# Two transformer-like blocks in one kernel: TensorE takes part of the expert row sums in the scan and in the routing, and the row units are dealt out anew

## What is computed

```
u = expert_u[eidx]
v = expert_v[eidx]
act = jax.nn.gelu(jnp.einsum('td,thkd->thk', xb, u).astype(jnp.float32), approximate=False)
return jnp.einsum('thk,thkd->td', (g * act).astype(v.dtype), v)
```

```
y_diag = jnp.einsum('blsgr,bsgrp->blgrp', cb[..., None] * decay, xc)
y_off = jnp.einsum('blgn,bgrpn->blgrp', cc, state) * jnp.exp(acum)[..., None]
new_state = (state * jnp.exp(acum[:, -1])[..., None, None]
             + jnp.einsum('blgn,blgr,blgrp->bgrpn', bc, to_end, xc))
```

## Time and profile before

| | |
|---|---|
| median of 3 runs | 3194.34 us (3190.66 to 3200.55) |
| the profiled execution: its time, its span | 3194.24 us, 3192.5 us |
| PE busy in the span | 2254.2 us |
| DVE busy | 1920.1 us |
| POOL busy, 1024 gathers of 0.52 MB | 1288.0 us |
| DMA moved | 807.66 MB, mean 253 GB/s |
| mean granted TensorE clock | 0.841 of 2.4 GHz |

### The profile page before, as it was taken

The page is one execution under the profiler, slowest core; times in us unless marked ns, Lnnn a source line. Parts: engine busy times, 40 slices in busy tenths (PEclk is TensorE's granted clock), DMA queues, the critical chain, the costliest instruction groups (busy, mean ns, idle before and its releaser), DMA issues. The chain is left out here.

```text
span 3192.5 us, 25912 instructions
## 1 busy us (share of the span) xinstructions
PE 2254.2 (71%) x8920; PEld 1652.1 (52%) x8920; DVE 1920.1 (60%) x3629; ACT 485.6 (15%) x1248; POOL 1288.0 (40%) x1058
## 2 busy tenths in 40 slices
PE   6987899753785568775745473135548957797998
PEld 5846788543653557663622362023347426564863
DVE  2317110288988995855799878996876681251000
ACT  3412100111321210001101101011011001231100
POOL 0000000004775464865357887886887550000000
...
GB/s 137 132 79 1 145 158 158 99 53 275 403 402 336 216 356 380 391 389 329 260 244 302 396 411 352 351 291 333 335 409 412 416 407 186 20 2 122 170 144 117
DMA packets 292402, 807.66 MB, mean 253 GB/s; under 512 B 35744, under 2 KB 52128, under 8 KB 292272
## 3 DMA queue, kind: packets, MB, share of 16 engines
...
HBM read 803.84 MB, written 2.10 MB: 252 GB/s over the span
## 5 line engine op out<-in xcount | busy, mean ns | idle before, releaser
L1021 POOL DMA_INDIRECT expert_rows<-in_peer_u,chosen x512 | 673.1, 1315 | 973.7 <-DVE chosen L1522 717.7
L1021 POOL DMA_INDIRECT expert_rows<-in_peer_v,chosen x512 | 611.5, 1194 | 355.0 <-DVE h L1103 143.1
L1093 DVE SCALAR_TENSOR_TENSOR expert_rows<-expert_rows,u 128x1024 f32<-128x1024 f32 x512 | 606.5, 1223 | 71.5 <-DMA expert_rows<-in_peer_u,chosen 65.7
L1103 DVE SCALAR_TENSOR_TENSOR h<-expert_rows,expert_coef,h 128x1024 f32<-128x1024 f32 x240 | 309.1, 1288 | 29.8 <-DMA expert_rows<-in_peer_v,chosen 27.4
L1103 DVE SCALAR_TENSOR_TENSOR u<-expert_rows,expert_coef,u 128x1024 f32<-128x1024 f32 x236 | 304.4, 1290 | 30.3 <-DMA expert_rows<-in_peer_v,chosen 30.0
L573 PE MATMUL product<-uT,in_slab 128*128 128x272 f32 (+1 forms) x1024 | 241.0, 391 | 94.8 <-DMA in_slab<-in_w_in 94.8
L573 PEld LDWEIGHTS product<-uT,in_slab 128*128 128x128 f32 x1024 | 193.6, 193 | 127.2 <-issue 92.6
L2219 PE MATMUL mlp_up<-mlp_xT,mlp_slab 128*128 128x256 f32 x1024 | 227.3, 385 | 16.1 <-DMA mlp_slab<-in_w_up 14.4
L2229 PE MATMUL mlp_down<-mlp_slab,upT 128*128 128x512 f32 x512 | 221.2, 593 | 4.2 <-DMA mlp_slab<-in_w_down 4.2
L2219 PEld LDWEIGHTS mlp_up<-mlp_xT,mlp_slab 128*128 128x128 f32 x1024 | 197.5, 193 | 45.7 <-DMA mlp_slab<-in_w_up 15.9
L1215 PE MATMUL mix_product<-uT,mix_slab 128*128 128x258 f32 (+1 forms) x768 | 173.4, 389 | 15.6 <-DMA mix_slab<-in_w_in 9.1
...
## 6 DMA issues: line engine op xcount, KB each, us to landing
...
```

Of the source, the lines that this page charges most:

```text
L1021: pool.indirect_dma_start(out=self.row(n), out_offset=None, in_=self.tables[0 if dot else 1], in_offset=bass.IndirectOffsetOnAxis(ap=picks ...
L1093: dve.scalar_tensor_tensor(self.row(n), self.row(n), 1.0, u, ALU.mult, ALU.mult, accum_out=dot).then_inc(self.rows_used, 1)
L1103: dve.scalar_tensor_tensor(o, self.row(n), coef, o, ALU.mult, ALU.add).then_inc(self.rows_used, 1)
```

## The change

The units of half 1's first block are dealt out anew: 128 in project (4 at each column tile instead of 3), 128 in scan (8 at each pass instead of 3), 128 in merge instead of 172, 8 in the norm instead of 12, 120 in route. PE takes 48 of the 128 adds of tile 0 (3 of 8, in scan) and 69 of the 128 adds of tile 1 (3 of 8 in the norm and the search, which is 27; then 6 of 8 in the pair search, which is 42), 117 in all instead of 32. The diagonals get six buffers of their own. In scan the two PSUM banks for PE's sums come from `cb` and `grown`: their two buffers now share a bank each, PE does the products with the state before `begin`, and two of its waits are one pass tighter. Half 0's first block and the whole second block keep their order.

```diff
-PLAN_ONE = (140, 60, 172, 12)
+PLAN_ONE = (128, 128, 128, 8)
...
             for n in range(CONV):
                 if bg:
-                    bg.use(dve, 3)
+                    bg.use(dve, 4)
                 dve.wait_ge(tap_ready, n + 1)
...
+        if bg:
+            bg.share_with_tensor(ctx, psum)
         sums = psum(ctx, "sums", [P, 512])
         seg = [psum(ctx, f"seg{i}", [P, HPG, P]) for i in range(2)]
-        cb = [psum(ctx, f"cb{i}", [P, 512]) for i in range(2)]
         yo = [psum(ctx, f"yo{i}", [P, 2, GW]) for i in range(2)]
-        grown = [sums, psum(ctx, "grown", [P, 512])]
+
+        if bg:
+            both = psum(ctx, "cb", [P, 512])
+            cb, grown = [both[:, i * P:(i + 1) * P] for i in range(2)], [sums[:, i * GW:(i + 1) * GW] for i in range(2)]
+        else:
+            cb = [psum(ctx, f"cb{i}", [P, 512])[:, 0:P] for i in range(2)]
+            grown = [x[:, 0:GW] for x in (sums, psum(ctx, "grown", [P, 512]))]
...
                 if q >= 2:
                     square_group(q - 2)
+                if bg:
+                    bg.diagonals(act, SETS_S + SETS_Q * q)
...
                 if bg:
-                    bg.use(dve, 3)
+                    bg.use(dve, SETS_Q)
...
                 if q >= 2:
                     pe.wait_ge(decay_done, q - 1)
                     pe.wait_ge(mixer_ready, q - 1)
+                if bg and q:
+                    pe.wait_ge(mixer_ready, q)
                 at = slice(M + c * P, M + (c + 1) * P)
-                pe.matmul(cb[q % 2][:, 0:P], bf[:, g, at], cf[:, g, at], start=True, stop=True)
+                pe.matmul(cb[q % 2], bf[:, g, at], cf[:, g, at], start=True, stop=True)
...
             for q in range(N + 1):
-                if q + 1 < N:
+                if q + 1 < N and not bg:
                     begin(q + 1)
                 if q < N:
                     c, g = q // GROUPS, q % GROUPS
@@ -949,14 +962,21 @@
 
...
                     if q >= 2:
                         pe.wait_ge(y_ready, q - 1)
-                    if FIRST + max(q - 1, 0):
-                        pe.wait_ge(state_done, FIRST + max(q - 1, 0))
+                    done = q if bg else FIRST + max(q - 1, 0)
+                    if done:
+                        pe.wait_ge(state_done, done)
                     pe.matmul(yo[q % 2][:, 1, :], cf[:, g, M + c * P:M + (c + 1) * P], state[:, g * GW:(g + 1) * GW],
                               start=True, stop=True)
-                    pe.matmul(grown[q % 2][:, 0:GW], bt[:, c, g * STATE:(g + 1) * STATE], product(xend, q),
+                    pe.matmul(grown[q % 2], bt[:, c, g * STATE:(g + 1) * STATE], product(xend, q),
                               start=True, stop=True).then_inc(off_done, 1)
+                if q + 1 < N and bg:
+                    begin(q + 1)
                 if q:
                     inside(q - 1)
+                if bg:
+                    bg.tensor_sums(pe, SETS_S + SETS_Q * q)
+            if bg:
+                bg.tensor_sums(pe, UNITS)
             leave(pe)
 
 UNITS = 2 * TT * SLOTS
...
     RING = 16
-    SHARE = 64
-
-    def __init__(self, nc, t, sem, ctx, block):
-        self.block = block
+    DIAGS = 6
+
+    IN_SCAN, IN_SEARCH, IN_PAIRS, SEARCH = (1, 3, 6), (1, 3, 6), (1, 2, 4, 5, 6, 7), 72
+
...
                                         "rows_used_by_pe", "diagonal_ready"))
-        self.tensor_units = [n for n in range(UNITS - self.SHARE, UNITS) if n % 2]
+        self.diag = ctx.enter_context(nc.sbuf_tensor("expert_diag", [P, self.DIAGS, P], F32, side="right"))
+        self.tensor_units = [n for n in range(SLOTS, 2 * SLOTS) if n % 8 in self.IN_SCAN]
+        self.tensor_units += [n for n in range(3 * SLOTS, 3 * SLOTS + self.SEARCH) if n % 8 in self.IN_SEARCH]
+        self.tensor_units += [n for n in range(3 * SLOTS + self.SEARCH, 4 * SLOTS) if n % 8 in self.IN_PAIRS]
...
     def plan(self, n):
 
-        self.goal = min(self.goal + n, UNITS * len(self.halves))
-
-    def share_with_tensor(self, ctx, psum, ident, room):
-
-        self.ident = ident
-        self.diag = [room[:, i * P:(i + 1) * P] for i in range(4)]
-        self.total = [psum(ctx, f"odd_sum{i}", [P, 512]) for i in range(2)]
+        self.base, self.goal = self.goal, min(self.goal + n, UNITS * len(self.halves))
+
+    def share_with_tensor(self, ctx, psum):
+
+        self.total = [psum(ctx, f"expert_sum{i}", [P, 512]) for i in range(2)]
 
     def diagonals(self, act, n):
...
     def diagonals(self, act, n):
 
-        for k in range(self.diags, self.diags + n):
+        end = self.by_tensor(min(self.base + n, self.goal))
+        for k in range(self.diags, end):
             half, _, m, at = self.place(self.tensor_units[k])
             act.wait_ge(self.coef_ready, half * TT + m + 1)
-            if k >= 4:
-                act.wait_ge(self.pe_used, k - 3)
-            act.activation(self.diag[k % 4], self.ident[:], ACT.Copy, scale=self.coef[:, m, at:at + 1]
+            if k >= self.DIAGS:
+                act.wait_ge(self.pe_used, k - self.DIAGS + 1)
+            act.activation(self.diag[:, k % self.DIAGS, :], self.ident[:], ACT.Copy, scale=self.coef[:, m, at:at + 1]
                            ).then_inc(self.diag_ready, 1)
-        self.diags += n
-
-    def odd_sums(self, pe, n):
-
-        for k in range(self.products, self.products + n):
+        self.diags = max(self.diags, end)
+
+    def tensor_sums(self, pe, n):
+
+        end = self.by_tensor(min(self.base + n, self.goal))
+        for k in range(self.products, end):
             unit = self.tensor_units[k]
+            tile = unit // SLOTS * SLOTS
             pe.wait_ge(self.landed[unit % self.RING], 16 * (unit // self.RING + 1))
             pe.wait_ge(self.diag_ready, k + 1)
             for side in range(2):
-                ins = pe.matmul(self.total[side][:], self.diag[k % 4], self.row(unit)[:, side * 512:(side + 1) * 512],
-                                start=k == 0, stop=k == len(self.tensor_units) - 1)
+                ins = pe.matmul(self.total[side][:], self.diag[:, k % self.DIAGS, :],
+                                self.row(unit)[:, side * 512:(side + 1) * 512],
+                                start=k == self.by_tensor(tile), stop=k == self.by_tensor(tile + SLOTS) - 1)
             ins.then_inc(self.pe_used, 1)
-        self.products += n
+        self.products = max(self.products, end)
 
     def activate(self, act):
 
@@ -1109,7 +1136,8 @@
         ins = dve.tensor_tensor(h, h, u, ALU.add)
         if shared:
...
             ins.then_inc(self.summed, 1)
-            dve.wait_ge(self.summed, 1)
+            self.sums += 1
+            dve.wait_ge(self.summed, self.sums)
             dve.wait_ge(self.pe_used, self.by_tensor(end))
...
+            if bg:
+                pe.wait_ge(bg.complete, 1)
             r = 0
...
-BG_MERGE = (50, 8, 8, 10, 6, 5)
+BG_MERGE = (36, 6, 6, 8, 4, 4)
...
                     if j:
                         score_tile(i, j - 1)
+                    if bg:
+                        bg.tensor_sums(pe, SETS_J * (8 * i + j))
                 score_tile(i, 7)
             if bg:
-                bg.odd_sums(pe, bg.SHARE // 2)
+                bg.tensor_sums(pe, UNITS)
             leave(pe)
 
...
                     if j:
                         drain_scores(i, j - 1)
+                    if bg:
+                        bg.diagonals(act, SETS_J * (8 * i + j))
                 drain_scores(i, 7)
             for m in range(TT):
                 if bg:
-                    bg.diagonals(act, (SETS_M[0] + SETS_M[1]) // 2 if m == 0 else sum(SETS_M) // 2)
+                    bg.diagonals(act, 16 * SETS_J + m * sum(SETS_M) + SETS_M[0] + SETS_M[1])
                 act.wait_ge(centred, m + 1)
                 act.activation(top_[:], top_[:], ACT.Exp).then_inc(exped, 1)
             if bg:
-                bg.diagonals(act, bg.SHARE // 2 - bg.diags)
+                bg.diagonals(act, UNITS)
             leave(act)
 
         @block.vector
...
-SETS_J, SETS_M = 4, (8, 8, 8, 8)
+SETS_S, SETS_Q, SETS_J, SETS_M = 5, 8, 4, (8, 8, 6, 6)
```

32 lines of the change are left out of this document (18 added, 14 removed).

## The result

The changed kernel takes 3233.98 us (median of 4 runs, 3225.42 to 3239.97), the kernel before 3193.22 beside it: ratio 1.0125, 95% interval 1.0095 to 1.0155. It is slower by 41 us, where I had forecast 5 us less. The profiled execution has a span of 3238.2 us.

The account below looks back on a forecast made before the run. DVE was taken to bound scan and route, the DMA merge, both meeting in project; 28 + 57 - 54 - 2 - 34 = -5 us gave 3189 us, own range 3169 to 3204, with rivals 8 in 10 between 3150 and 3232.

Parts of the forecast that it names:

- Project, +28: Project: four dots per tile lengthen DVE's pitch from 4.90 to 6.04 us, so the stage ends at 1011 instead of 983.
- Both are more than 412, so both live on the ring's lead; I add 3 us: Project: the DMA must give 434 GB/s, 429 before; prefetched units cover what exceeds 412, for 3 us more.
- Scan, +57: Scan: sum of +14 for adds, +5.5 at section ends, +31 for DVE waiting on `inside`, +6 for clock.
- the 6 us for the lower clock: Scan: allowance of +6 us for some stretches in which PE runs at 1.2 GHz.
- Merge, -54: Merge: 48 fewer units save 25.2 MB, 61 us at 412 GB/s, not all won; stage 297 us.
- 3 us of slack: Merge: allowance of 3 us on top of phases priced at 412 GB/s, giving 297 us.
- Norm and route, -2 and -34: Norm: fewer dots in DVE, -2 us. Route: head 0, search -18, pair search -16, sum -34 us.
- what I named as the sign: Route: pair search would take 93 us, with DVE waiting for PE at its end.
- The gain survives: Rival, chance 0.20: project's DMA-bound end stays near 983 (-28) or merge loses all 61 us (-7); about 3155 us.
- PE did not bound scan: Denies the rival, chance 0.19, that PE at 1.2 GHz takes 18.8 us per scan pass; 3240 us with half of 15.
- The handshake: Rival, chance 0.05: in scan `inside` overtakes the wait, so DVE's 31 us of waiting go; 3158 us.
- Route gave what was forecast: Denies the rival, chance 0.11, that PE's sums hold the ring and route gives nothing, +34; 3223 us.

Follow-up runs that it names:

- e6: Changed kernel with project's four dots laid between the taps and half of each slab loaded from the third on (stale weights); project 247.2 us, read for project alone.
- e2: Changed kernel with the four dots of each project tile laid between its taps, same instructions and bytes; 3235.67 us, ratio 1.0115 to the kernel before.
- e5: Changed kernel loading only half of each slab from project's third on (stale weights), dots in unchanged order; project 264.2 us, read for project alone.
- e1: Changed kernel with three dots instead of four ahead of each project tile's taps, plan still 128; 3193.27 us, ratio 0.9991 to the kernel before.
- e3: Changed kernel with PE's `inside` of the previous pass moved ahead of `begin` of the next in scan; 3232.76 us, ratio 1.0107 to the kernel before.
- e9: Changed kernel with merge's deal of units set to (56, 5, 5, 5, 2, 2) for (36, 6, 6, 8, 4, 4); 3238.72 us, ratio 1.0122 to the kernel before.
- e4: Kernel before with only the new route, 128 units there; plan, project, scan and merge as before; 3187.64 us, ratio 0.9971 to the kernel before.

## Why the prediction was wrong, by its own steps

- **Project, +28, measured +46: the step that failed.** The pitch of 6.04 us, the z part's dependence on the last tile and its length were right: 977.8 to 1027.5 is 49.7 us, and the sum has 1011 less 963, 48. What failed is "Both are more than 412, so both live on the ring's lead; I add 3 us". The last tap came 15 us later than the 963 which that gives. First, the DMA gives 403 GB/s in this stage and not the 412 of merge's best stretch, and 2.62 MB per tile at 403 is 6.5 us; e6, against e2, shows that the waits vanish with the bytes cut. Second, the sum has no term for POOL, which is a term put at nothing without a reason. The trace of before had what was needed: its gathers last 0.94 to 1.68 us under three dots, and the reserve is 0.60 us a tile. Four dots in a row made gathers of 1.98, 1.99 and 1.14 us and turned that reserve into a deficit, 3 gathers where DVE uses 4. With one limit taken away the other leaves 11.4 or 12.1 of the 17.2 us of waits (e5, e2), with both taken away none (e6).
- The Trainium skill has a rule that bears on the second limit, in "SBUF — State Buffer", section "SBUF: two separate sides": GpSimd can't write the descriptors of its DMAs while a VectorE instruction of certain kinds holds the port pair that they share. The trace agrees, on the dots and on the taps, also of two inputs in SBUF: the gather's end lies 0.81 us behind the dot's end (804.91), and as far behind the end of the tile's last tap (808.64, tap's end 807.84). That it is the port by which they are held no run shows. I did not draw on that page; it would have given a rival.
- **The choice of the sign.** I wrote "The 32 dots that lay behind the taps, beside the z part, are gone, but the z part never waited for them", and counted their removal as no gain. It is a loss: they were what the DMA worked for during the z part (406 GB/s in e1, 84 in after). e1, with them, gives all 46 us back: 28 of these I had in the sum already, as longer pitches, but in DVE's time alone and not in the DMA's.
- **Scan, +57, measured +57.** Shown by e3: the order of `begin` and `inside` is what DVE waits for. The term for it was 31 and was 34.9, in 14 passes. DVE's busy time rose by 19.9 us (150.6 to 170.4), for which the sum had 16.5. That leaves little of the 6 us for the lower clock (it was 0.89, for 0.74 before); what the clock cost no run shows. The total is right partly by errors that cancel.
- **Merge, -54, measured -40**, and -31 to -34 in e1 to e3. The mechanism was right and the size off. The term that is too small is the "3 us of slack": the phases are priced at 412 GB/s, as if a phase's units could always be fetched in it. DVE ran out of units for 54 us; the DMA was at 150 and 249 GB/s for 20 us each, which at 412 is about 21 us lost, an estimate from these two rows. e9 closed this hole, another one opened, and merge was 3.7 us shorter; what the rest of the miss is stays open.
- **Norm and route, -2 and -34, measured -2.5 and -34.5**, but route's total is right by errors that cancel. Head 0, measured -3; search -18, measured -9 (118.7 for 128): the sum has no wait of PE for ACT's diagonals, and there are 13.7 us of it; pair search -16, measured -22, which is the 87 us that DVE's own sum gave. DVE does not wait for PE at the end, contrary to what I named as the sign; it does in e4, with eight units more in the pair search.
- **Second block, 0.** In the profiled execution +19, with a scatter of 6 at least; open.
- **The rivals.** "The gain survives" was the furthest off: project's DMA share went from 1.00 to 0.90. PE did not bound scan (clock 0.89, e3). The handshake was not hidden, and e3 shows that hiding it would not have given the 31 us of that rival: 10.8 in scan, and nothing to be seen in the whole time. Route gave what was forecast. What came true was none of the rivals: the DMA left without requests. The 3234 us lie 2 us above the 3150 to 3232 that the prediction gave to forecast and rivals together.
